# Three pairs of groups per feed-forward stage from seven block products, with two of the four slab sums made by adding transfers

## The reference

```python
def swiglu_ffn(h, w_gate, w_up, w_down):
    return (jax.nn.silu(h @ w_gate) * (h @ w_up)) @ w_down
...
    for layer in range(DEPTH):
        h = rmsnorm(x, norm_mix_g[layer])
        ...
        x = x + y
        h = rmsnorm(x, norm_ffn_g[layer])
        x = x + swiglu_ffn(h, ffn_w_gate[layer], ffn_w_up[layer], ffn_w_down[layer])
```

## Time and profile before

| | |
|---|---|
| Time before, median of 3 runs | 716.3 us (716.2 to 716.61) |
| The profiled execution, its own time | 715.99 us |
| Its span | 714.1 us |
| TensorE busy | 701.0 us (98%) |
| VectorE busy | 586.1 us (82%) |
| ScalarE busy | 422.6 us (59%) |
| Bytes moved | 158.41 MB, mean 222 GB/s |

### The profile page before, as it was taken

The page is one execution under the profiler, slowest core; times in us unless marked ns, Lnnn a source line. Parts: engine busy times, 40 slices in busy tenths (PEclk is TensorE's granted clock), DMA queues, the critical chain, the costliest instruction groups (busy, mean ns, idle before and its releaser), DMA issues.

```text
span 714.1 us, 9602 instructions
## 1 busy us (share of the span) xinstructions
PE 701.0 (98%) x3764; PEld 609.7 (85%) x3764; DVE 586.1 (82%) x879; ACT 422.6 (59%) x640; POOL 12.4 (2%) x18
## 2 busy tenths in 40 slices
PE   7999999999999999999999999999999999999996
PEld 6888889989999999888788888888888888888885
DVE  5879999798976889988889688875698896888744
ACT  3156535974775768778845546364667455463623
POOL 0000000000220001000000000000000000000000
PEclk8999999999999999999999999999999999999998
DMA  8999996499935338534704860776345047607501
GB/s 333 417 421 417 422 405 268 175 378 345 391 119 212 145 128 264 138 119 177 265 31 148 324 235 1 307 282 235 119 178 214 22 156 315 236 0 295 176 1 60
DMA packets 23469, 158.41 MB, mean 222 GB/s; under 512 B 2624, under 2 KB 2880, under 8 KB 5248
## 3 DMA queue, kind: packets, MB, share of 16 engines
q1 hardware_dynamic: 22464, 152.82, 55.4%
q0 software_dynamic: 960, 4.98, 2.6%
HBM read 156.74 MB, written 1.05 MB: 221 GB/s over the span
## 4 chain that ended last, share of the span: by engine, by line
PE 80%; DVE 11%; ACT 7%; issue 1%; DMA 1%; SPq 0%; DVEq 0%
PE pb L1909 19%; PE pb L1911 19%; PE pb L1910 19%; PE pb L1981 14%; DVE w L1238 4%; DVE raw L1241 3%; PE pb L2228 2%; PE pb L2333 1%; ACT w L796 1%; PE pb L2451 1%; DMA x<-x_dram 1%; ACT t L914 1%; DVE f L1238 1%; ACT r L911 1%; DVE r L1238 1%
## 5 line engine op out<-in xcount | busy, mean ns | idle before, releaser
L1238 DVE TENSOR_TENSOR w<-raw,w 128x2048 fp32r<-128x2048 f32 x91 | 206.9, 2285 | 55.0 <-ACT w L796 55.0
L796 ACT ACTIVATE w<-raw 128x2048 fp32r<-128x2048 f32 x95 | 179.3, 1911 | 59.2 <-PE pb L1911 29.4
L1909 PE MATMUL pb<-w,r 128*128 128x512 f32 (+1 forms) x528 | 207.2, 392 | 1.7 <-DVE t L1241 1.4
L1911 PE MATMUL pb<-w,r 128*128 128x512 f32 (+1 forms) x528 | 204.2, 387 | 0.0
L1910 PE MATMUL pb<-w,r 128*128 128x512 f32 (+1 forms) x528 | 203.9, 386 | 0.0
L1909 PEld LDWEIGHTS pb<-w,r 128*128 128x128 f32 x528 | 99.2, 188 | 23.4 <-issue 2.0
L1911 PEld LDWEIGHTS pb<-w,r 128*128 128x128 f32 x528 | 99.1, 188 | 20.5
L1910 PEld LDWEIGHTS pb<-w,r 128*128 128x128 f32 x528 | 99.3, 188 | 19.1
L1909 PE MATMUL pb<-r,w 128*128 128x256 f32 x288 | 82.5, 287 | 0.3 <-DVE r L1238 0.3
L1911 PE MATMUL pb<-r,w 128*128 128x256 f32 x288 | 81.5, 283 | 0.0
L1910 PE MATMUL pb<-r,w 128*128 128x256 f32 x288 | 81.5, 283 | 0.0
(11 more groups left out here) (232 smaller groups left out, 916.2 us busy)
## 6 DMA issues: line engine op xcount, KB each, us to landing
raw<-w_dram SPq DMA_DIRECT2D x125, 1024.0 KB, 6.2
ow<-w_dram SPq DMA_DIRECT2D x8, 1024.0 KB, 16.2
ow<-w_dram SPq DMA_DIRECT2D x8, 512.0 KB, 16.8
f<-w_dram SPq DMA_DIRECT2D x4, 1024.0 KB, 7.6
oh<-w_dram SPq DMA_DIRECT2D x2, 1024.0 KB, 23.6
w<-w_dram POOLq DMA_DIRECT2D x2, 1024.0 KB, 14.8
x<-x_dram SPq DMA_DIRECT2D x2, 512.0 KB, 5.6
acc<-row_dram POOLq DMA_DIRECT2D x2, 512.0 KB, 3.9
```

Source lines behind the costliest of these rows:

```text
L796: return e.activation(out, in_, ACT.Copy, **kw)
L1238: return e.tensor_tensor(out, a, b, op)
L1909: e.matmul(out, a_hi, b_hi, start=start, stop=False)
L1911: return e.matmul(out, a_lo, b_hi, start=False, stop=stop)
```

## The change

- PAIRS becomes (3, 6, 9): singles 0, 1, 2, pair 3 and 4, single 5, pair 6 and 7, single 8, pair 9 and 10. LAST becomes 9 and 10, and the last pair takes the branch in which "h" stands ahead of the down slab.
- The slab 11 is loaded twice: as kind "chain" into the chain buffer, at the head of the pair, and behind the top slab as kind "11" into the ring, from where it is split. Splits of "11" no longer read the chain buffer.
- The sums e and f leave VectorE. GpSimd issues two transfers that add for each pair (`slab_sums`): chain += top, when the chain slab has landed, and top += low (both read again from memory), when top has landed. Their semaphores are s_sume and s_sumf; ScalarE's copies of e and f wait for them. VectorE still makes g and h.
- ScalarE's and VectorE's programs for a pair have some lines in another order: ScalarE's copies ("fill") are ahead of gates by one place; VectorE makes t ahead of the low half of slab k + 7, and in the last pair splits slab k + 10 behind the last `hidden`, with k the place of "11".

```diff
--- before.py
+++ after.py
@@ -10,7 +10,7 @@
 
 
 NG = FF // 256
-PAIRS = (3, 7)
+PAIRS = (3, 6, 9)
 UNITS_OF = [("two" if i in PAIRS else "one", i) for i in range(NG) if i - 1 not in PAIRS]
 SEVEN = ("11", "21", "e", "g", "f", "22", "h")
 LAST = [NG - 2, NG - 1] if UNITS_OF[-1][0] == "two" else [NG - 1]
@@ -73,8 +73,9 @@
                 if i >= 2:
                     plan.append(("down", "ffn_w_down_2", layer, i - 2))
                 continue
+            plan.append(("chain", None, layer, 0, i))
+            plan.append(("part", None, layer, 0, i + 1))
             plan.append(("11", None, layer, 0, i))
-            plan.append(("part", None, layer, 0, i + 1))
             plan.append(("21", None, layer, 4, i))
             plan.append(("part", None, layer, 4, i + 1))
             plan.extend(("form", name, layer, i) for name in ("e", "g"))
@@ -111,8 +112,8 @@
 PLAN = slab_plan()
 
 OWN = [i for i, p in enumerate(PLAN) if p[0] in ("u", "g", "y") or p[0] == "heads" and p[1] != "pool_map_2"]
-RING = [i for i in range(len(PLAN)) if i not in OWN and PLAN[i][0] not in ("11", "form")]
-MATS = [i for i in range(len(PLAN)) if i not in OWN and PLAN[i][0] not in ("first", "mod", "part")]
+RING = [i for i in range(len(PLAN)) if i not in OWN and PLAN[i][0] not in ("chain", "form")]
+MATS = [i for i in range(len(PLAN)) if i not in OWN and PLAN[i][0] not in ("first", "mod", "part", "chain")]
 MODS = [i for i in RING if PLAN[i][0] == "mod"]
 
 UNITS = [("mod_b", 8, "norm_g", 0), ("mod_b", 0, None, 0), ("mod_b", 16, None, 0),
@@ -154,7 +155,7 @@
     return len(PAIRS) * layer + PAIRS.index(i)
 
 
-def part(layer, k0, i):
+def part_of(layer, k0, i):
 
     return PLAN.index(("part", None, layer, k0, i + 1))
 
@@ -464,8 +465,8 @@
 
         s_hi, s_lo, s_mod, s_half, s_minus = (sem(f"s_{n}") for n in ("hi", "lo", "mod", "half", "minus"))
         s_sum = {k: sem(f"s_sum{k}") for k in BY_DMA}
-        s_ch, s_form, s_blk, s_bhi, s_blo, s_snap, s_fork = (
-            sem(f"s_{n}") for n in ("ch", "form", "blk", "bhi", "blo", "snap", "fork"))
+        s_ch, s_sume, s_sumf, s_form, s_blk, s_bhi, s_blo, s_snap, s_fork = (
+            sem(f"s_{n}") for n in ("ch", "sume", "sumf", "form", "blk", "bhi", "blo", "snap", "fork"))
 
         s_ps = sem("s_ps")
 
@@ -597,23 +598,24 @@
             return s_raw[n % NRAW], 16 * (n // NRAW + 1)
 
         def form_made(name, layer, i):
-            return s_form, 4 * pair_at(layer, i) + ("e", "g", "f", "h").index(name) + 1
+            q = pair_at(layer, i)
+            if name in ("e", "f"):
+                return (s_sume if name == "e" else s_sumf), 16 * (q + 1)
+            return s_form, 2 * q + ("g", "h").index(name) + 1
 
         def there(i):
 
             kind, name, layer, *at_ = PLAN[i]
-            if kind == "11":
-                return s_ch, 16 * (pair_at(layer, at_[1]) + 1)
             if kind == "form" and name == "22":
-                return landed(part(layer, 4, at_[0]))
+                return landed(part_of(layer, 4, at_[0]))
             return form_made(name, layer, at_[0]) if kind == "form" else landed(i)
 
         def raw_of(i):
             kind, name, *at_ = PLAN[i]
-            if kind == "11" or kind == "form" and name in ("e", "g", "h"):
+            if kind == "form" and name in ("e", "g", "h"):
                 return chain
             if kind == "form":
-                i = part(at_[0], 0 if name == "f" else 4, at_[1])
+                i = part_of(at_[0], 0 if name == "f" else 4, at_[1])
             return raw[RING.index(i) % NRAW]
 
         def emptied_at(i):
@@ -718,7 +720,7 @@
                 n = width(i)
                 if slab[0] == "form":
                     continue
-                if slab[0] == "11":
+                if slab[0] == "chain":
                     q = pair_at(slab[2], slab[4])
                     if q == 0:
                         p.wait_ge(*ended("fm", 3))
@@ -784,8 +786,20 @@
             e.dma_start(prow[:, :], row_d[0]).then_inc(s_prow, 16)
             e.wait_ge(s_cv3, 1)
             e.dma_start(frow[:, :], row_d[1]).then_inc(s_frow, 16)
+
+            def slab_sums(layer, i):
+                p, low_ = part_of(layer, 0, i), part_of(layer, 4, i)
+                e.wait_ge(s_ch, 16 * (pair_at(layer, i) + 1))
+                e.dma_start(chain, w_d[p], accum_op=ADD).then_inc(s_sume, 16)
+                e.wait_ge(*landed(p))
+                e.dma_start(raw_of(p)[:, :], w_d[low_], accum_op=ADD).then_inc(s_sumf, 16)
+
+            for i in PAIRS:
+                slab_sums(0, i)
             e.wait_ge(s_lo, LOW_AT[AT["h", 0, PAIRS[-1]]])
             e.dma_start(rc, rcnt_d).then_inc(s_rc, 16)
+            for i in PAIRS:
+                slab_sums(1, i)
 
         @block.scalar
         def _(e):
@@ -1176,15 +1190,15 @@
                         snap(layer, i)
                         fill(k + 1)
                         fill(k + 2)
+                        fill(k + 3)
                         gates(layer, i, [0])
                         hidden_high(layer, i - 1)
-                        fill(k + 3)
                         fill(k + 4)
                         fill(k + 5)
+                        fill(k + 6)
                         gates(layer, i + 1, [1])
-                        fill(k + 6)
+                        fill(k + 7)
                         gates(layer, i + 1, [0])
-                        fill(k + 7)
                         gates(layer, i, [1])
                         fill(k + 8)
                         continue
@@ -1288,24 +1302,17 @@
                     w = W[(k + 2) % NSPL]
                     p.wait_ge(s_hi, k + 1)
                     tt_(w[:, 1, 0:n], raw_of(i)[:, 0:n], w[:, 0, 0:n].bitcast(f32), SUB).then_inc(s_lo, 1)
-                    if PLAN[i][0] in ("11", "form"):
+                    if PLAN[i][0] == "form":
                         form_sums(k, *PLAN[i])
 
             def form_sums(k, kind, name, layer, *at_):
 
                 g = at_[-1]
-                if kind == "11":
-                    top = part(layer, 0, g)
-                    p.wait_ge(*landed(top))
-                    p.wait_ge(s_lo, LOW_AT[k])
-                    tt_(chain, chain, raw_of(top)[:, :], ADD).then_inc(s_form, 1)
-                elif name == "e":
-                    top, low_ = part(layer, 0, g), part(layer, 4, g)
+                if name == "e":
+                    low_ = part_of(layer, 4, g)
                     p.wait_ge(*landed(low_))
                     p.wait_ge(s_lo, LOW_AT[k])
                     tt_(chain, chain, raw_of(low_)[:, :], ADD).then_inc(s_form, 1)
-                    p.wait_ge(*form_made("e", layer, g))
-                    tt_(raw_of(top)[:, :], raw_of(top)[:, :], raw_of(low_)[:, :], ADD).then_inc(s_form, 1)
                 elif name == "22":
                     own_ = PLAN.index(("21", None, layer, 4, g))
                     p.wait_ge(s_lo, LOW_AT[AT["g", layer, g]])
@@ -1824,18 +1831,20 @@
                         hidden_low(layer, i - 1)
                         fill(k + 3)
                         made_from(layer, i, "u2", "c11")
+                        made_from(layer, i, "t", "u2")
                         fill(k + 4)
-                        made_from(layer, i, "t", "u2")
                         fill(k + 5)
                         made_from(layer, i, "u3", "t")
                         made_from(layer, i, "c22", "t")
                         fill(k + 6)
                         hidden(layer, i + 1, [1])
                         made_from(layer, i, "c12", "c22")
-                        fill(k + 7)
+                        if i + 2 < NG:
+                            fill(k + 7)
                         hidden(layer, i + 1, [0])
                         made_from(layer, i, "c21", "u3")
                         hidden(layer, i, [1])
+                        fill(k + 7)
                         fill(k + 8)
                         continue
                     k = AT["gu", layer, i]
@@ -2503,7 +2512,7 @@
             continue
         if p[0] == "form":
             continue
-        if p[0] in ("gu", "11", "21", "part"):
+        if p[0] in ("gu", "11", "21", "part", "chain"):
             _, _, layer, k0, g = p
             rows, some = slice(k0 * P, (k0 + 4) * P), slice(g * 256, g * 256 + 256)
             m = np.concatenate([a["ffn_w_gate_2"][layer][rows, some], a["ffn_w_up_2"][layer][rows, some]], 1)
```

## The result

The changed kernel takes 722.63 us (median of 6 runs, 720.71 to 725.9), the kernel before 716.22 (715.84 to 716.61): ratio 1.0093, interval 1.0071 to 1.0116. It is slower by 6.4 us; the forecast was 715.6. The profiled execution is the slowest of the six, 725.9 us with a span of 724.1. Six executions of one program spread over 5 us, those of the kernel before over 0.8; that is part of the result.

A forecast was written before the change was run, and what follows sets the result against it. Both feed-forward stages were taken as bound by TensorE's matmuls: -5.44 - 1.07 - 0.1 (pauses) + 2 x 2.2 (tail stalls) + 1.5 (pool split) = -0.7 us, so 716.3 becomes 715.6, range 711.0 to 719.8.

The forecast's parts named there:

- the step of 0.227 us: Feed-forward stages on TensorE: time per 512-column matmul, from 24 matmuls of a down slab in 5.44 us.
- 5.44 us for 24 matmuls: Both feed-forward stages: six pairs in place of four remove 24 matmuls on TensorE, 5.44 us less.
- the 1.1 us for the stalls behind the transposes: Units behind pairs: four late TensorE starts of 0.27 us go when ScalarE's copies come ahead of gates, 1.1 us gain.
- sums e and f nearly free on VectorE: Pairs: removing f saves VectorE 0.15 us, not 2.3; removing e saves more but nothing waits for it.
- the tail stall: Last pair, 9 and 10, of each stage: TensorE waits for VectorE from 27.7 to 29.9, 2.2 us.
- the pool split behind it: First stage only: slab 10 and pool splits precede the transposed groups' low halves, so TensorE waits 1.5 us.
- the distance between two pairs: Within a stage: the next pair starts on TensorE 47.9 us after the pair before.
- sum e late: Slower rival, pairs 6 and 9: the transfer for e lands up to 2.9 us late, giving 722; chance 0.20.
- sign that the prediction named as wrong: In the profile after: DMA as the releaser of ScalarE's copies for e, or no stall at the tail.
- Slab 21, loaded beside the sums: Next pair's load: lands at 38 to 41, wanted at 37.8; ScalarE's gates late under 1 us, taken as nothing.
- The rival at 0.05: Slower rival, TensorE's clock: half clock for 7 us behind the tail stall, 3.5 us per stage, 722.6; chance 0.05.
- Nearer to the wait that did nothing: Tail stall of 2.2 us judged nearer to 1.4 us waits at full clock than to the 3.2 us wait before half clock.

The follow-up runs named there:

- the best kernel: Changed kernel with sums e and f on VectorE, and in the last pair the slab 10 copy behind gates and transposed groups' copies, c21 earlier: 710.5 us.
- without the adding traffic: Changed kernel with the twelve adding transfers cut to 128 of 2048 columns, output differs: 716.36 us, ratio 1.0002.
- the twin kernels: Changed kernel, 722.63 us, and the same with sums e and f back on VectorE and no adding transfers, 717.19 us.
- the better tail order: Changed kernel, adding transfers kept, last pair with slab 10's copy behind gates and transposed groups' copies, c21 earlier: 715.52 us, ratio 0.9995.
- the tail order: Changed kernel, last pair: slab 9's low half behind the last gate product, transposed groups' low halves ahead of slabs 10 and pool: 718.37 us.
- the filler: Kernel with the sums on VectorE plus nine unused 512-column matmuls on TensorE in the tail stall: 715.73 us, ratio 0.9996.

## Why the prediction was wrong

**Right**, each by a run: the step of 0.227 us and 5.44 us for 24 matmuls, and the 1.1 us for the stalls behind the transposes (the best kernel has both, to 1 us); sums e and f nearly free on VectorE; the tail stall and the pool split behind it, by place and size (2.1 and 1.5 us without the adding traffic, forecast 2.2 and 1.5); the distance between two pairs (forecast 47.9, though its terms add to 47.75; 47.6 us without the adding traffic). Sum e did not hold anything up: ScalarE's copy of e was never released by it. It was no comfortable margin, though. Ahead of pair 9 it landed at 44.9 us from pair 6's start, near the far end of the forecast 40.7 to 45.8, and was covered by the lateness of slab 21. So the slower rival as it was told, "sum e late", did not happen, though its time, 722, is the measured one; that the number fits is luck. Neither sign that the prediction named as wrong (a DMA as the releaser of copies for e, no stall at the tail) came, so its signs could not show this failure.

**The step that failed** is the sentence "Slab 21, loaded beside the sums, lands at 38 to 41 and is wanted at 37.8; ScalarE then does the gates late by under 1 us, taken as nothing." Three things were wrong in it.

- The landing. ScalarE's copies of slab 21, released by its landing, started at 42.5 us from pair 3's start (370.99) and at 44.8 from pair 6's. Slab low landed 19.5 us after its issue, against 15.2 in the earlier trace rows. I had costed the two transfers by when they land and not by what they take: they keep the DMA engines full at 279 to 293 GB/s while five plain loads of the next pair are due.
- What stands behind it. Not only ScalarE's gates: VectorE's low half of 21 and two gate products also come ahead of the low half of e. It came 2.85 us late in pair 6 and 3.3 in pair 9, and then it is on VectorE's path, which the prediction itself had shown to have no gap up to the tail.
- The next pair. The late pair 6 frees the chain buffer at 26.0 in place of 21.9, and all loads of pair 9 start from there. Without the adding traffic it was 22.4.

The delay went into waits inside the pairs (3.8 us in all) and into the tail stall (3.3 in place of 2.1, twice). Price by the twin kernels: 5.4 us (717.19 to 722.63, beside kernels before of 716.1 and 716.2), and 5.0 with the better tail order.

**The clock.** The rival at 0.05 happened in part. Behind 3.2 us of waiting at the start the clock had halved; behind a wait of 3.3 us it did in one stage of the profiled run and not in the other (with f on VectorE in both, 0.57), behind 2.1 us in one stage each of three kernels, behind 2.3 us with the tail order in none. "Nearer to the wait that did nothing" was the wrong choice. In the kernel with the sums on VectorE six of ten runs lie above 717, with the filler none above 716.05, and the medians differ by 1.5 us. How much of the 5 us of spread in the changed kernel is the clock stays open: its slowest run (725.9) and its quickest (720.71) have the same mean granted clock, 0.992.

**Sum.** Measured less forecast is 7.0 us. The transfers are 5.4 of it. The other 1.6 is what the twin without them lies above the forecast, and the filler, which keeps the clock up, takes 1.5 of that back.

**The range** ended at 719.8, though the prediction had priced a delay at 722. It gave that price a chance only on the condition that sum e is late, and gave none to slab 21 late by itself.

## What to carry to other kernels

Before handing an engine's sum to a transfer that adds, look at whether the engine waits there anyway, and count all transfers that are due in the same stretch at the adding rate: the plain load behind it pays, not the transfer itself. Follow what a late pair frees late, too, since the next pair's loads wait for it. When two engines hand small pieces to each other, put the large copies that nothing waits for behind the small ones at the place where no work follows; here the last pair's order alone, with the stretch at half clock that went with its stall, was worth more than the removed matmuls (717.2 to 710.5 against 5.4). A stall of TensorE of 2 us or more should be costed with a stretch at half clock behind it in a part of the executions, as here.

## What the runs showed of the hardware

Adding transfers held the DMA engines full (share 1.03 to 1.04) at 279 to 293 GB/s; plain ones of the same bytes ran at 426, and the packets of their queue took about half the time. The Trainium skill ("DMA: Bandwidth & Descriptors", section "Queues, rings and completion order") has an engine take turns between queues; the landings of plain loads at 15 to 19.5 us beside the sums agree. Turns alone do not explain them: beside plain copies in the same queue the loads landed after 11.4 us at the median, so it is what each adding packet takes in its turn. The clock halved behind waits of 2.1 and 3.3 us in one stage of a profiled execution and not in the other (0.53 and 0.50 against 1.00).
